# Two-column post-norm factors, unread products in six waits, and shifted head and gate times in a four-layer transformer kernel on one Trainium2 core

## The reference

```
def first_block(x, ...):                       # layer 0: mixer_ab, layer 1: mixer_cd
    for layer in range(2):
        h = rms_norm(x, mix_pre_g[layer]);  m = mixer(h)
        x = x + rms_norm(m, mix_post_g[layer])
        h = rms_norm(x, ffn_pre_g[layer]);  f = channel_mixer(h)
        x = x + rms_norm(f, ffn_post_g[layer])
def second_block(x, ...):
    for l in range(2): x = hybrid_layer(x, l, ...)
    return rms_norm_2(x, final_norm_g)
def hybrid_layer(x, l, ...):
    p = split(rms_norm_2(x, norm_g) @ w_in)     # fox, diff, moba, gla: 4 heads of 128 each
    fox, moba = attention * silu(gate)
    diff = rms_norm_2(differential attention) * const * silu(gate)
    gla  = rms_norm_2(gated linear attention) * silu(gate)
    return x + concat(fox, diff, moba, gla) @ w_out
```

## Time and profile before

| | |
|---|---|
| device time, median of 3 runs | 2840.71 us (2835.01 to 2843.76) |
| the profiled execution | 2837.55 us, of it span 2835.7 us |
| PE | 2749.1 us busy, 97% of the span |
| DVE | 1945.8 us busy, 69% |
| ACT | 1379.4 us busy, 49% |
| POOL | 518.3 us busy, 18% |
| DMA | 482.61 MB, mean 170 GB/s |
| chain that ended last | PE 90%, DVE 5%, ACT 2%, POOL 2%, issue 1% |

### The profile page before, as it was taken

The page is one execution under the profiler, slowest core; times in us unless marked ns, Lnnn a source line. Parts: engine busy times, 40 slices in busy tenths (PEclk is TensorE's granted clock), DMA queues, the critical chain, the costliest instruction groups (busy, mean ns, idle before and its releaser), DMA issues.

```text
span 2835.7 us, 50169 instructions
## 1 busy us (share of the span) xinstructions
PE 2749.1 (97%) x18314; PEld 2484.2 (88%) x18314; DVE 1945.8 (69%) x2757; ACT 1379.4 (49%) x1931; POOL 518.3 (18%) x487
## 2 busy tenths in 40 slices
PE   8999999999999999999999999999999999999998
PEld 8998988888888899988888888899878889987887
DVE  6675678777744787678777754676667766666775
ACT  5434555554544557555555444453445454344553
POOL 1150025444411000023444411000000020000001
PEclk9999999999999999999999999999999999999999
DMA  7455445555555455445555555444544555554454
GB/s 253 156 176 182 151 147 178 187 183 187 187 188 185 140 168 164 134 142 171 185 185 185 185 187 186 153 163 161 179 144 149 168 182 173 165 176 143 148 170 141
DMA packets 132569, 482.61 MB, mean 170 GB/s; under 512 B 15040, under 2 KB 15296, under 8 KB 132288
## 3 DMA queue, kind: packets, MB, share of 16 engines
q1 hardware_dynamic: 130608, 475.06, 51.1%
q10 hardware_dynamic: 1808, 5.39, 0.6%
HBM read 477.25 MB, written 2.10 MB: 169 GB/s over the span
## 4 chain that ended last, share of the span: by engine, by line
PE 90%; DVE 5%; ACT 2%; POOL 2%; issue 1%; DMA 0%; DVEq 0%; ACTq 0%; POOLq 0%
PE BANK L462 32%; PE BANK L457 28%; PE BANK L463 16%; PE BANK L478 8%; DVE WLO L1324 1%; PE BANK L839 1%; PE BANK L532 1%; ACT WHI L890 1%; PE BANK L469 1%; PE BANK L829 1%; PE BANK L849 0%; POOL M L2058 0%; DVE TM L1346 0%; PE BANK L676 0%; POOL M L2061 0%
## 5 line engine op out<-in xcount | busy, mean ns | idle before, releaser
L1324 DVE TENSOR_TENSOR WLO<-RING,WHI 128x1024 fp32r<-128x1024 f32 x902 | 1112.9, 1236 | 664.5 <-ACT WHI L890 657.7
L890 ACT ACTIVATE WHI<-RING 128x1024 fp32r<-128x1024 f32 x902 | 954.0, 1059 | 1144.4 <-PE BANK L463 636.2
L462 PE MATMUL BANK<-H,WHI 128*128 128x512 f32 x2560 | 917.8, 403 | 14.7 <-DVE H L1334 9.8
L457 PE MATMUL BANK<-H,WHI 128*128 128x256 f32 x4160 | 764.8, 286 | 22.3 <-DVE H L1334 19.0
L463 PE MATMUL BANK<-H,WLO 128*128 128x256 f32 x2560 | 719.8, 281 | 0.0
L457 PEld LDWEIGHTS BANK<-H,WHI 128*128 128x128 f32 x4160 | 653.2, 193 | 28.9 <-issue 23.2
L462 PEld LDWEIGHTS BANK<-H,WHI 128*128 128x128 f32 x2560 | 483.0, 189 | 136.0 <-issue 15.3
L457 PE MATMUL BANK<-H,WLO 128*128 128x256 f32 x2080 | 590.2, 284 | 0.0
L462 PE MATMUL BANK<-BIGR,WHI 128*128 128x512 f32 x1536 | 539.9, 396 | 3.4 <-DVE BIGR L1957 3.4
L463 PEld LDWEIGHTS BANK<-H,WLO 128*128 128x128 f32 x2560 | 485.5, 190 | 1.7 <-issue 1.0
L463 PE MATMUL BANK<-BIGR,WLO 128*128 128x256 f32 x1536 | 431.0, 281 | 0.0
(11 more groups left out here) (281 smaller groups left out, 2348.3 us busy)
## 6 DMA issues: line engine op xcount, KB each, us to landing
RING<-w SPq DMA_DIRECT2D x902, 512.0 KB, 3.3
X<-xT ACTq DMA_DIRECT2D x4, 512.0 KB, 9.9
outT<-M SPq DMA_DIRECT2D x3, 512.0 KB, 2.9
TB<-tab ACTq DMA_DIRECT2D x1, 1216.5 KB, 5.5
V<-vec ACTq DMA_DIRECT2D x1, 644.0 KB, 8.6
TM<-BIG ACTq DMA_DIRECT2D x16, 32.0 KB
TM<-BIG ACTq DMA_DIRECT2D x8, 64.0 KB
outT<-M SPq DMA_DIRECT2D x2, 256.0 KB, 3.2
```

The lines of the kernel that those rows point to most:

```text
L457: last = mm(bank[:, 0:T], wt[s][:, kk, :], x, start=start and n == 0, stop=stop and n == 2)
L462: mm(bank[:, :], WHI[s][:, kk, :], both, start=start, stop=False)
L890: A(WHI[at % SPLIT][:, :, :], RING[at % RAW][:, :].rearrange("p (k n) -> p k n", k=UB), ACT.Copy)\
L1324: TT(WLO[at % SPLIT][:, :, :], RING[at % RAW][:, :].rearrange("p (k n) -> p k n", k=UB), WHI[at % SPLIT][:, :, :].bitcast(f32), ALU.subtra ...
```

## The change

It has four parts, which are independent of one another.

A. **Factors by token.** `sums_by_token` multiplies the squares (as the stationary operand, 128 tokens at a time) with one column of ones, so that the sums come out as 2 columns, a token in each partition. The mean, root and reciprocal work on 128x2. DVE multiplies the identity with them (two diagonals, 128x256), and `spread` multiplies all-ones with that, which gives the factor of each token in every partition of a PSUM bank; `lead` reads the factor there.
B. **Unread products.** `occupy` issues products of the identity with ones (256 columns) that nobody reads: 2 before `spread` and 5 after it in each of the four leads, 6 before the queries' first wait, 7 before the first wait for the LRU's output.
C. **Hybrid times.** gla heads, diff heads, moba heads and the norm of diff start one or two ticks later on all engines, the fox heads where they did. The norm of diff spreads over more ticks. The gates come in five parts, moba in two, at ticks 98, 113, 115 and 119 on ACT and one later on DVE (the last behind all gates), with one more tick between the halves of a gate. The wait for the mean of gla's norm moves from before diff's first scores to before diff's first transposes.
D. **PSUM waits.** The first outputs behind a value product, and the first quad of a value product, wait for other counts of `bank_free`.

```diff
-        GATE_AT = {"gla": 98, "fox": 106, "diff": 114}
+        GATES = (("gla", 0, 4), ("fox", 0, 4), ("diff", 0, 4), ("moba", 0, 2), ("moba", 2, 4))
+        GATE_AT = (98, 113, 115, 119)
+        MIXED_STARTS = (0, 4, 8, 12, 14)
...
+            def occupy(bank, n):
+                for _ in range(n):
+                    mm(bank[:, 0:T], ident, tcol("ones", T), start=True, stop=True)
...
             def run_q(r):
-                    pe.wait_ge(sem("bank_free"), o0 + 4 * max(quad - 1, 0))
+                    pe.wait_ge(sem("bank_free"), o0 + 4 * (quad - 1) if quad else o0 - 2)
...
             def lead(r, u0, o0):
                 pe.wait_ge(sem("bank_free"), o0)
+                if u0:
+                    occupy(banks[0], 2)
+                    spread(BANK[o0 % BANKS])
+                    occupy(banks[0], 5)
...
+            def sums_by_token():
+                at = lambda t: BANK[7][:, T + t:T + t + 1]
+                tokens_of = lambda tile, t: TM[:, tile, t * P:(t + 1) * P]
+                pe.wait_ge(sem("sq_added"), 15 * step_no(c, "added"))
+                mm(at(0), tokens_of(4, 0), ones[:, 0:1], start=True, stop=False)
+                pe.wait_ge(sem("sq_done"), 16 * step_no(c, "event"))
+                mm(at(0), tokens_of(3, 0), ones[:, 0:1], start=False, stop=True)
+                mm(at(1), tokens_of(4, 1), ones[:, 0:1], start=True, stop=False)
+                mm(at(1), tokens_of(3, 1), ones[:, 0:1], start=False, stop=True).then_inc(sem("summed"), 1)
+            def spread(bank):
+                pe.wait_ge(sem("diagonal"), step_no(c, "diagonal"))
+                mm(bank[:, 0:T], ones, TM[:, 11, :], start=True, stop=True).then_inc(sem("spread"), 1)
...
-                    if not isinstance(i, int) or o >= BANKS and not (led and i == 1 and j < BANKS - 1):
+                    if r in (RUN_POOLED, RUN_GATES) and isinstance(i, int) and i == 0:
+                        pe.wait_ge(sem("bank_free"), o0 - 4 if j < 2 else o0 + 1)
+                    elif not isinstance(i, int) or o >= BANKS and not (led and i == 1 and j < BANKS - 1):
                         pe.wait_ge(sem("bank_free"), o - (BANKS - 1))
...
                             if r.src == "LRU" and isinstance(i, int) and i == 0 and j == 0:
+                                if k == 0:
+                                    occupy(BANK[o0 % BANKS], 7)
...
             def queries():
+                pe.wait_ge(sem("bank_free"), c["output"] - (BANKS - 1))
+                occupy(BANK[c["output"] % BANKS], 6)
...
-                    later(62, heads("fox", l, o0 + 13, o0 + 33)), later(74, gla_heads(l, o0 + 29)),
-                    later(78, heads("diff", l, o0 + 21, o0 + 41)), later(102, heads("moba", l, o0 + 29, o0 + 45)),
-                    later(103, head_norm(M[:, 4:8, :], (BANK[5], BANK[5]))))
+                    later(62, heads("fox", l, o0 + 13, o0 + 33)), later(76, gla_heads(l, o0 + 29)),
+                    later(80, heads("diff", l, o0 + 21, o0 + 41)), later(104, heads("moba", l, o0 + 29, o0 + 45)),
+                    later(105, head_norm(M[:, 4:8, :], (BANK[5], BANK[5]))))
...
             def post_norm(name, l, pre, pl):          # DVE
-                mean(D_MODEL, TM[:, 10, :])
-                reciprocal(TM[:, 10, :])
+                TS(small(MEAN_COL, 2), BANK[7][:, T:T + 2], 1.0 / D_MODEL, EPS, ALU.mult, ALU.add).then_inc(sem("mean_sq"), 1)
+                dve.wait_ge(sem("root"), step_no(c, "rstd"))
+                then(v.reciprocal(small(RECIP_COL, 2), small(ROOT_COL, 2)))
+                TT(TM[:, 11, :]..., ident..., small(RECIP_COL, 2)..., ALU.mult).then_inc(sem("diagonal"), 1)
...
             def gate(n, l):                            # DVE
+                yield
+                yield
                 dve.wait_ge(sem("mixed_hi"), done)
```

83 lines of the change are left out of this document (47 added, 36 removed).

## The result

The changed kernel takes 2811.46 us (median of 4 runs, 2805.61 to 2812.66), the kernel before 2841.47 us (4 runs, 2835.01 to 2843.76): ratio 0.9894, interval 0.9872 to 0.9916. The profiled executions are 24.9 us apart (span 2835.7 before, 2810.8 after), less than the medians' 30.0. Of the 5.1 us between the two figures, 3.9 stand on the side of before, whose profiled execution (2837.55) is that much under its median, and 1.2 on the side of the change (2812.66 over 2811.46). The account by stages goes by the traces, where 24.9 us are to be placed.

The account below looks back on a forecast made before the run. PE was taken to bound the kernel, busy 2749.1 of 2835.7 us; gains of 2.6 + 5.2 + 1.7 + 0.6 + 20.0 + 4.3 = 34.4 us off the 2840.7 median gave 2806. Range 2797 to 2821.

Parts of the forecast that it names:

- rival 2: Hybrid layers: the stall moves, DVE's backlog costing PE 7.2 us a layer where 2.5 was left; time 2815.5, chance 0.18.
- A, the factors: Four leads: a shorter factor chain saves 0.65 us a lead, 2.6 in all; bounds 0 and 1.0 a lead.
- B, leads: Four leads: unread products fit in PE's wait and bring back the full clock, 5.2 us; bounds 0 and 6.6.
- B, queries and LRU: Fillers inside the waits there cost nothing and return the clock: 1.7 us at the queries, 0.6 at the LRU.
- C, hybrid layers: Two hybrid layers: new times remove PE's waits and half clock, 10.0 us a layer, 20.0 for both.
- D, PSUM waits: L478's 2.6 and L462's 1.7 us waits for banks the next work doesn't write first all go: 4.3 us.
- 0.65 a lead: In each lead: factor chain 0.76 us shorter, less 0.12 charged for the one-column sums.
- rivals 4 and 6: Leads' 64 PSUM factor products: 4, 0.07 us dearer each, 2810.5, chance 0.08; 6, 0.67 us each, 2849, chance 0.03.
- Rival 1: Leads, queries, LRU: fillers don't hold the clock and stick out some 1.5 us a lead; time 2820, chance 0.12.
- 2.5 left of 12.5: Each hybrid layer: PE waits 1.5 to 2.2 us once and 0.5 at the output product, leaving 2.5 us.
- The output product under 0.6: Changed profile, hybrid layers: PE's wait at the output product was to be under 0.6 us.
- if the half clock returns behind the fillers: Sign of being wrong: no clock near 0.5 was expected behind the leads, the queries and the LRU.

Follow-up runs that it names:

- experiment 1: The changed kernel without any unread products (part B undone); 2813.05 us, ratio 0.9944 to the kernel before.
- experiment 2: The changed kernel with the wide factors of before (part A undone), all fillers kept directly behind the sums; 2812.02 us, ratio 0.9933 to the kernel before.
- experiment 9: The changed kernel with wide factors (part A undone) and 1, 3, 4 and 3 more unread products ahead of the wide sums; 2805.02 us, ratio 0.9937.
- experiment 8: The changed kernel with 1, 3, 4 and 3 more unread products ahead of the one-column sums of the four post-norms; 2799.85 us, ratio 0.9872.
- experiment 3: The changed kernel with the hybrid layers' times, gates and norm waits of before (part C undone); 2821.04 us, ratio 0.9961 to the kernel before.
- experiment 4: The changed kernel with the PSUM waits of before (part D undone); 2811.12 us, ratio 0.994 to the kernel before.
- experiment 10: The changed kernel with the additions of experiment 8 and 6, first moba gate's product one tick earlier on DVE, one tick less between moba gate halves; 2793.14 us.
- Experiments 5: The changed kernel without three of the four reciprocals of diff's norm in each hybrid layer, their values left out of the computation; one time, 2798.84 us.
- 6: The changed kernel with the reciprocals of diff's norm one tick earlier on DVE; 2803.88 us, ratio 0.9889 to the kernel before.
- 7: The kernel of experiment 6 with the gate of the fox heads one tick earlier too (112 in place of 113); 2809.76 us, ratio 0.9915.

## Why the prediction was right, and where its steps were off

The time, 2811.5, lies between the 2806 forecast and the 2815.5 of rival 2, and the gain by the traces, 24.9, is rival 2's 25.0. That the last two agree is chance: rival 2 kept A and the clock's return whole. Against the 34.4 of the sum the traces have 72%. The mechanisms were right in kind, and two terms of the sum were too large: C by 7.65, and A by 2.0 as the traces stand, by at least 0.5 with their scatter. Term by term:

```
term                          forecast   measured
A, the factors                  2.6        0.6, scatter -0.1 to 2.1 (3.5 where the clock holds on both sides)
B, leads                        5.2        5.0, scatter 4.3 to 6.5
B, queries and LRU              1.7 + 0.6  2.39 + 0.33
C, hybrid layers               20.0       12.35, scatter 1.2 a layer
D, PSUM waits                   4.3        5.8
```

The measured column is what undoing each part cost; its rows overlap, and their sum isn't the change's 24.9. For B the overlap is plain at the queries: their stretch is 3.4 us long before and 6.8 in experiment 1, so undoing B costs 2.39 there, where the change gained 1.46, and at the LRU 0.20. The section on the change calls its parts independent; in time A and B are not, since in the leads A is worth more with the clock held.

A smaller error runs through the sum. It takes half of PE's time at half clock as loss. By the changed kernel's trace a pair of products, L467 and L468, follows the last one after 0.35 us at full and 0.64 us at half clock:

```profile
2207.70 0.40 PE L467 MATMUL BANK<-H,WHI 128*128 128x512 f32 x1
...
2208.05 0.40 PE L467 MATMUL BANK<-H,WHI 128*128 128x512 f32 x1
...
2225.94 0.63 PE L467 MATMUL BANK<-BIGR,WHI 128*128 128x512 f32 x1
...
2226.58 0.63 PE L467 MATMUL BANK<-BIGR,WHI 128*128 128x512 f32 x1
```

So 45% of that time is loss, 1.5 us of a full 3.4. The queries' 1.7 was measured as 1.46.

**A's chain was right, its worth was not.** The timeline of the first post-norm after the change, the answer to the earlier trace rows:

```profile
385.86 0.16 DVE L1558 TENSOR_SCALAR SMALL<-BANK 128x2 f32<-128x2 f32 x1 [1.43 <-PE BANK L566]
386.29 0.17 DVE L1560 RECIPROCAL SMALL<-SMALL 128x2 f32<-128x2 f32 x1 [0.27 <-ACT SMALL L1108]
386.49 0.42 DVE L1561 TENSOR_TENSOR TM<-TB,SMALL 128x256 f32<-128x256 f32 x1
...
387.71 0.48 DVE L1417 SCALAR_TENSOR_TENSOR TM<-M,V,BANK 128x256 f32<-128x256 f32 x1 [0.79 <-PE BANK L571]
```

From 385.86 to 387.71 are 1.85 us (1.94 forecast, 2.70 before). The failed step is that 0.65 a lead was added to the clock's return as if the two were independent. Without B, A only moves work into the half-clock stretch (experiment 1). With B and the narrow sums the clock falls in three leads of four, and in 16 of 24 over all traces with this code; with B and the wide sums in one of four (experiment 2), and in another one of four in experiment 9. Ahead of the narrow sums PE waits 0.45, 1.18, 1.97 and 1.18 us in the four leads, and the falls are 1, 5, 6 and 4 of six. When experiment 8 fills these waits it gets both the shorter chain and the clock. Whether it is the waits or the narrow products that let the clock fall was not tested apart.

**The bank as a source costs nothing.** L1417's durations in the changed kernel (ns min/median/max):

```profile
L1417 DVE SCALAR_TENSOR_TENSOR TM<-M,V,BANK x64: 468/474/481, 387.7 to 1840.7; 128x256 f32<-128x256 f32 x64
```

474 ns against 480 for L1376, so L1780's row was the right guide and rivals 4 and 6 are out. The Trainium skill ("VectorE: DVE Perf Modes", the TRN2 errata) would have had 65 ns more; these 64 products don't show it.

**B's fillers fit, and held the clock in one lead of four.** In lead 1 `spread` and the five behind it take 386.97 to 389.83 and the lead's first product starts at 389.86: no room was left. In lead 2 they run at half clock. PE's timeline of that lead (start, duration, line, count):

```profile
942.58 0.38 PE L564 MATMUL BANK<-TB,TM 128*128 128x1 f32 x2 [1.18 <-ACT TM L1051]
...
943.27 1.14 PE L492 MATMUL BANK<-TB 128*128 128x256 f32 x4
944.55 1.22 PE L571 MATMUL BANK<-TM,TB 128*128 128x256 f32 x2
945.57 3.35 PE L492 MATMUL BANK<-TB 128*128 128x256 f32 x10
```

`spread` takes 1.22 us (0.70 in lead 1, below) and the five behind it 3.35 (2.32), together 1.55 us longer, about what rival 1 said, 1.5 a lead, and the tiles of the lead are at full clock again behind them. Rival 1 came true for three leads in its place but not in its price: it left the queries and the LRU whole, and of the leads it took 1.0 to 1.75, as experiment 8 gave back. In lead 2 that is the clock alone: experiment 3, without the fillers of 8 but with the clock held there, has the same 1.23.

```profile
386.97 0.70 PE L571 MATMUL BANK<-TM,TB 128*128 128x256 f32 x2 [0.17 <-DVE TM L1561]
387.51 2.32 PE L492 MATMUL BANK<-TB 128*128 128x256 f32 x10
```

Lead 1 had no half clock in the changed kernel and one at 387.8 us in experiment 4, with the same instructions there; leads 2 and 4 differ likewise between traces of one code. So fillers of this size make the fall of the clock rarer but don't decide it, and nothing in the traces here says which execution is spared. The Trainium skill ("TensorE: Matmul & The Clock Gate", Part 1) says that the activity is watched in windows that run freely, and these runs agree as far as they go: the same instructions met half clock in one execution and not in another.

**C, the failed step.** "I expect PE to wait 1.5 to 2.2 us once, and 0.5 at the output product: 2.5 left of 12.5." The removal was right, by the waits: gla's 2.4 and diff's 1.0 a layer are gone and moba's 4.0 is 0.8, with no half clock in the middle of either layer. The new order's end was not. DVE in the first layer's end after the change:

```profile
2206.44 1.74 DVE L1850 RECIPROCAL M<-M 128x256 f32<-128x256 f32 x1
2208.21 1.28 DVE L1854 SCALAR_TENSOR_TENSOR BIG<-M,V 128x1024 f32<-128x1024 f32 x1
2209.53 1.23 DVE L2005 TENSOR_TENSOR BIGR<-BIG,BIGR 128x1024 fp32r<-128x1024 f32 x1
2210.67 1.22 DVE L2000 SCALAR_TENSOR_TENSOR BIG<-BIG 128x1024 f32<-128x1024 f32 x1
...
2217.33 2.35 DVE L1363 TENSOR_TENSOR WLO<-RING,WHI 128x1024 fp32r<-128x1024 f32 x2
2219.60 0.68 DVE L2000 SCALAR_TENSOR_TENSOR BIG<-BIG 128x512 f32<-128x512 f32 x1
...
2224.38 0.69 DVE L2005 TENSOR_TENSOR BIGR<-BIG,BIGR 128x512 fp32r<-128x512 f32 x1 [0.70 <-ACT BIGR L1323]
```

and PE's waits there:

```profile
2214.14 0.49 PE L467 MATMUL BANK<-H,WHI 128*128 128x512 f32 x1 [0.97 <-DVE WLO L1363]
...
2223.14 0.50 PE L467 MATMUL BANK<-BIGR,WHI 128*128 128x512 f32 x1 [1.80 <-DVE BIGR L2005]
...
2225.13 0.80 PE L467 MATMUL BANK<-BIGR,WHI 128*128 128x512 f32 x1 [1.02 <-DVE BIGR L2005]
```

The backlog of DVE came as worked out; the wait for the low part was 0.97, under my 1.5 to 2.2. What I left out is that a backlog which PE's buffers hide from the weights isn't hidden from the gates: the moba gate's product stood ready behind silu from 2215.4, but its turn came at 2219.60, behind two low parts, a gate half and an evacuation. Behind the two gate waits, 2.8 us together, stands a half-clock stretch of 6.8 us in the first layer and 3.4 in the second. The prediction had looked for one only behind a single wait of 2.4 us. The length of a single wait doesn't decide it: wherever these two waits stand a stretch follows them, but in experiment 10 one stands behind 1.98 us and none behind 2.43.

Left were 0.97 + 1.80 + 1.02, some 0.8 at moba's values, and half of 5.87 and 3.40: 7.5 and 6.3 a layer, not 2.5; it is rival 2's price (7.2) at another place, the output product instead of the weights. Experiments 5 and 6 show that the backlog is 2.1 of the 3.8 us. The rest, 1.7, did not go when 10 moved moba's gates in DVE's queue. That it is the chain from the last outputs through silu, product, high and low part is the rival that is left; it is argued and not shown, as no run shortened this chain. How to be rid of the rest I didn't find.

**D** was under-priced by the cost of a wait beyond its idle row (experiment 4), 0.26 to 0.30 us at each of five places, 1.4 in all. The wait of 0.50 at the pooled product (for `H`, L1987) stayed.

**What the profile was to show.** The chain near 1.9, L1417 at 0.48, the waits of gla, diff and moba under 1 us, and D's waits gone: right. The wait for L1363 was 0.97 where 1.5 to 2.2 was said. No half clock behind the leads: wrong for three, where it stands on `spread` and the fillers. The output product under 0.6: wrong. By its own sign, "if the half clock returns behind the fillers", the account of the leads had failed even though the time came out within the range.

## What to carry to other kernels

A shorter chain in front of a half-clock stretch is worth little until the clock is held (0.45 us for 3.2 in experiment 1, 3.5 with the clock held): price the two together, by how much of the stretch falls on work. When work is moved off one engine's critical wait, follow that engine's queue to the next thing that has no buffer; here the weights had 6 us of lead and the gates none. Compare such kernels by the start of the same unit of a fixed stream in two traces: stages without half clock then repeat to 0.03 us where medians of the whole differ by ten. But look at the clock of each stage in several executions of one code before a difference of 1 us is put down to an edit.

## What the runs showed of the hardware

**Two paces of the same stream.** In stretches where PE never waits and the clock reads 1.00 throughout, the same code ran at one of two paces. Units 200 to 300 in the first feed-forward part, before:

```profile
616.77 1.06 ACT L890 ACTIVATE WHI<-RING 128x1024 fp32r<-128x1024 f32 x1 [1.27 <-PE BANK L463]
...
899.44 1.06 ACT L890 ACTIVATE WHI<-RING 128x1024 fp32r<-128x1024 f32 x1 [1.77 <-PE BANK L463]
```

and in the kernel of experiment 4, whose code is the same there:

```profile
612.40 1.06 ACT L926 ACTIVATE WHI<-RING 128x1024 fp32r<-128x1024 f32 x1 [1.22 <-PE BANK L468]
...
889.73 1.06 ACT L926 ACTIVATE WHI<-RING 128x1024 fp32r<-128x1024 f32 x1 [1.71 <-PE BANK L468]
```

282.7 against 277.3 us for 100 units, 1.9%. A whole feed-forward part (units 140 to 315, and 421 to 590) is 9.3 or 9.1 us shorter at the faster pace, always by that amount or not at all; the executions profiled had none (before, after, 6, 7), one (1, 2, 3, 5, 8) or both (4, 9, 10). This fits the lumps, some 9 us apart, in which the runs of one kernel stand: of the profiled executions, those with both parts fast are among the fastest of their kernel's runs (4, 9, 10), and the one of before, with none, took 2837.55 us, as the slowest lump did. Some runs of the changed kernel, 2805.6 among them, may be of another pace than those of before; the runs without a trace can't show it. The pace doesn't explain why the result's runs of before lie up to 6 us over the profiled execution, which has no fast part. Two shorter stretches vary as well, with PE never waiting: units 725 to 800 take 1.4 us longer than before in eight of the ten experiments (not in 4 and 9), and the last 21 units 1.1 us longer in seven. What sets the pace is open: no run here changed it on purpose.

**A wait costs more than its row.** 0.26 to 0.30 us each, beyond the idle time, in five places of experiment 4.

**The same code meets the clock or doesn't.** Six traces with the same leads have 16 half-clock stretches in 24 leads; the two with three or four more unread products ahead of the sums of leads 2 to 4, and one ahead of lead 1's, have none in eight.
